# TensorE waits for its own last chunk, and makes a few narrow products, in every second up-projection chunk

## The reference

```python
for l in range(DEPTH):
    x = _layer_norm(DN_ALPHA * x + 0.5 * _swiglu(x, ffn1_w1[l], ffn1_w2[l]), ln1_g[l], ln1_b[l])
    mix = _token_mix(x, ...)
    x = _layer_norm(DN_ALPHA * x + mix, ln2_g[l], ln2_b[l])
    x = _layer_norm(DN_ALPHA * x + 0.5 * _swiglu(x, ffn2_w1[l], ffn2_w2[l]), ln3_g[l], ln3_b[l])
```

## Time and profile before

| | us |
|---|---|
| median of three runs | 2385.51 |
| lowest and highest | 2382.72, 2387.91 |
| profiled execution | 2399.49 |
| its span, first to last instruction | 2397.7 |
| TensorE busy | 2310.4 |
| VectorE busy | 1498.1 |
| ScalarE busy | 1190.8 |
| GpSimd busy | 244.1 |

### The profile page before, as it was taken

One profiled execution on the slowest core, in us unless ns is written; L12 is line 12 of the kernel. 1 busy time (PEld: TensorE's weight loads), 2 busy tenths in 40 slices (PEclk: granted clock), 3 DMA queues, 4 the chain that ended last, 5 costly groups with the idle time before them and its releaser, 6 DMA issues. The chain is left out here.

```text
span 2397.7 us, 45036 instructions
## 1 busy us (share of the span) xinstructions
PE 2310.4 (96%) x17296; PEld 2080.9 (87%) x17296; DVE 1498.1 (62%) x2663; ACT 1190.8 (50%) x1934; POOL 244.1 (10%) x272
## 2 busy tenths in 40 slices
PE   6999999999989999999999899999999998999998
PEld 4777677778878689999988899999999988999998
DVE  5487874453568875655476766655655578567654
ACT  6244743543345556434366555533534466555443
POOL 0012000000012000023010100121122001000320
PEclk9999999999999999999999999999999999999999
DMA  7321023444233035455554335455455454344552
GB/s 288 120 75 58 2 106 141 160 156 158 88 121 115 19 137 180 176 197 189 192 168 156 134 133 193 153 182 193 151 182 193 149 199 136 135 165 147 205 193 88
DMA packets 61844, 355.61 MB, mean 148 GB/s; under 512 B 6208, under 2 KB 19712, under 8 KB 20352
## 3 DMA queue, kind: packets, MB, share of 16 engines
q1 hardware_dynamic: 61552, 353.55, 41.0%
q10 hardware_dynamic: 144, 0.01, 0.0%
HBM read 349.29 MB, written 1.10 MB: 146 GB/s over the span
## 5 line engine op out<-in xcount | busy, mean ns | idle before, releaser
L240 DVE TENSOR_TENSOR w_lo<-ring,w_hi 128x1024 fp32r<-128x1024 f32 x638 | 811.9, 1305 | 454.7 <-ACT w_hi L226 454.3
L282 PE MATMUL psum<-x_hi,w_hi 128*128 128x256 f32 (+1 forms) x3376 | 1028.3, 305 | 13.2 <-DVE x_lo L579 3.6
L283 PE MATMUL psum<-x_lo,w_hi 128*128 128x256 f32 (+1 forms) x3376 | 1009.0, 299 | 0.0
L284 PE MATMUL psum<-x_hi,w_lo 128*128 128x256 f32 (+1 forms) x3376 | 1008.7, 299 | 0.0
L226 ACT ACTIVATE w_hi<-ring 128x1024 fp32r<-128x1024 f32 (+1 forms) x638 | 643.9, 1049 | 312.0 <-PE psum L284 145.5
L282 PEld LDWEIGHTS psum<-x_hi,w_hi 128*128 128x128 f32 x3376 | 638.1, 189 | 51.9 <-issue 12.0
L283 PEld LDWEIGHTS psum<-x_lo,w_hi 128*128 128x128 f32 x3376 | 636.7, 189 | 27.2 <-issue 1.7
L284 PEld LDWEIGHTS psum<-x_hi,w_lo 128*128 128x128 f32 x3376 | 635.3, 188 | 26.3
L1871 PE MATMUL psum<-h_hi,w_hi 128*128 (+1 forms) x640 | 179.0, 280 | 0.0
L1873 PE MATMUL psum<-h_lo,w_hi 128*128 (+1 forms) x640 | 179.0, 280 | 0.0
L1874 PE MATMUL psum<-h_hi,w_lo 128*128 (+1 forms) x640 | 179.0, 280 | 0.0
(11 more groups left out here) (332 smaller groups left out, 2859.1 us busy)
## 6 DMA issues: line engine op xcount, KB each, us to landing
ring<-wstream SPq DMA_DIRECT2D x320, 1024.0 KB, 4.8
x<-xT SPq DMA_DIRECT2D x2, 1024.0 KB, 7.7
x<-ctxT SPq DMA_DIRECT2D x2, 1024.0 KB, 10.2
rel_bias<-bias_by_distance SPq DMA_DIRECT2D x2, 1024.0 KB, 7.6
fox_bias<-forgetting_sums SPq DMA_DIRECT2D x2, 1024.0 KB, 7.5
cst<-consts SPq DMA_DIRECT2D x1, 1534.0 KB, 11.7
wk<-wk_once SPq DMA_DIRECT2D x8, 128.0 KB, 4.3
kk_sw<-kk_sw SPq DMA_DIRECT2D x8, 128.0 KB, 5.8
```

The lines of the kernel that those rows point to most:

```text
L240: dve.tensor_tensor(w_lo[:, c % 2, h], ring[:, (c + 2 * i) % RING, h], w_hi[:, c % 2, h].bitcast(F32), ALU.subtract).then_inc(split_done.s ...
L282: pe.matmul(o, w_hi[:, c, w_cols], hi, start=first, stop=False)
L283: pe.matmul(o, w_hi[:, c, w_cols], lo, start=False, stop=False)
L284: return pe.matmul(o, w_lo[:, c, w_cols], hi, start=False, stop=last)
```

## The change

In each up-chunk with s = 1 that `pe_columns` makes, TensorE waits, behind its two usual waits, until `chunk_done` counts its own chunk before. Then it makes `narrow` products of 32 columns with the first weight tile of the chunk and the first 32 tokens, into the accumulator's first 32 columns, which the first real product overwrites. `narrow` is 0 and 1 for the two feed-forward stages of the first layer and 2 and 3 for those of the second. Chunks with s = 0 and all other users of `pe_columns` get `None`, and for them nothing changes.

```diff
+NARROW = 32
...
-        def pe_columns(pe, i, s, hi, lo, tok, kt=KT, before=None, out=None, half_read=None):
+        def pe_columns(pe, i, s, hi, lo, tok, kt=KT, before=None, out=None, half_read=None, narrow=None):
...
                     if before and m == 0:
                         before(k)
+                    if narrow is not None and n == 0:
+                        pe.wait_ge(chunk_done.sem, g0[0] + s + 2 * i)
+                        for _ in range(narrow):
+                            pe.matmul(out[:, 0:NARROW], w_hi[:, c, 0:P], hi(0)[:, 0:NARROW], start=True, stop=True)
                     mm = three(pe, out[:, m * tok:m * tok + tok], slice(n * P, n * P + P), c, hi(k), lo(k), k == 0,
                                k == kt - 1)
...
-        def ffn_stage(layer, norm, more=True, bias=None):
+        def ffn_stage(layer, norm, more=True, bias=None, narrow=0):
...
-                                pe_columns(pe, i, s, hi, lo, S)
+                                pe_columns(pe, i, s, hi, lo, S, narrow=narrow if s else None)
...
-            ffn_stage(layer, layer_norm(layer - 1, 3) if layer else None, bias=None if layer else RelBias())
+            ffn_stage(layer, layer_norm(layer - 1, 3) if layer else None, bias=None if layer else RelBias(),
+                      narrow=2 * layer)
             mix_stage(layer)
-            ffn_stage(layer, layer_norm(layer, 2), layer < DEPTH - 1)
+            ffn_stage(layer, layer_norm(layer, 2), layer < DEPTH - 1, narrow=2 * layer + 1)
```

## The result

| | before | after |
|---|---|---|
| median of three runs, us | 2385.51 | 2410.89 |
| lowest and highest | 2382.72, 2387.91 | 2410.23, 2410.97 |
| profiled execution | 2399.49 | 2410.23 |
| its span | 2397.7 | 2408.5 |
| TensorE busy, products | 2310.4, 17296 | 2315.8, 17362 |

The change costs 25.4 us: ratio 1.0102, 95% interval 1.0067 to 1.0137. Forecast were 2407 (2389 to 2418), slower at 0.82.

What follows compares the result with a forecast made beforehand. TensorE, without a gap in the feed-forward stages, was taken to bound the kernel. To the median 2385.5 us were added 14.5 for waits and 7.3 for narrow products, with three long stages before and after: 2407.3, range 2389 to 2418.

Steps and rivals of the forecast that it cites:

- TensorE alone sets the end, and what is put into its queue is paid in full: Feed-forward stages: TensorE has no gap over 1584 products, about 180 to 187 us, so added work lengthens the stage.
- A wait costs 0.33 us: Up-chunks with s = 1: 44 waits at 0.33 us, 14.5 us together, ends 13.6 and 16.7.
- A narrow product costs 0.11 us: Behind the waits: 66 products paced by their loads at 0.11 us, 7.3 us together, ends 7.1 and 7.8.
- the 11 waits of one stage mostly come out alike: Feed-forward stages: supposed because each wait repeats the same sequence; a change of pace is worth 6.9 us a stage.
- a pace that varies from chunk to chunk within a stage: Feed-forward stages in the profile after: one of the signs named as showing the prediction wrong.
- Six in ten for long: Each feed-forward stage after the change: chance of the long pace, 0.1178 us a product against 0.1133.
- Three stages at the long pace before and three after: Four feed-forward stages: number of long ones unchanged, which one being indifferent, giving 2407.3 us; three long has chance 0.31.
- The first, waits that shake stages into the short pace: Feed-forward stages: two long 2400.4 us (chance 0.26), one 2393.5 (0.10), none 2386.6 (0.05).
- the fourth's two halves: Wait dearer, from 0.38 us, or timed runs before shorter-paced, from the 14 us: 2418 and more; "dearer" has chance 0.07.
- The second, all long: All four feed-forward stages become long, the fourth too: 2414.2 us, chance 0.11.
- The third, a pace below 0.1133: Feed-forward streams lock to 0.112 us a product, giving back 28.7 us: 2378.6, faster; chance 0.10.
- The fifth: The waits do nothing, the semaphore being always there before TensorE asks: 2385.5 + 7.3 us; given no chance.

Runs made afterwards that it cites:

- the four narrow products once: Kernel before plus four products of 32 columns, without a wait, ahead of one early chunk of each feed-forward stage; 2393.87 us, ratio 1.0028.

## Why the prediction was right, and where it wasn't

**TensorE alone sets the end, and what is put into its queue is paid in full: right.** All thirteen sums above charge every wait and every product at its full price. VectorE's and ScalarE's busy times differ from before by 0.3 and 1.1 us.

**A wait costs 0.33 us: right.** The hole is 0.33 in the earlier trace rows's counterpart after, and the third product behind it is late by 0.32 to 0.33, from a range of 0.31 to 0.38. That the new wait is met by the last product alone, and so stands nearer to ScalarE's release in the earlier trace rows than to the load in the earlier trace rows, held in the loop. In pairs that are written out the load came 0.39 to 0.40 after the last product, at the slow bound that the prediction took from the earlier trace rows, and the wait cost 0.40; those are five of 44.

**A narrow product costs 0.11 us: right.** The loads of the 66 are 0.108 to 0.112 apart, as those in the earlier trace rows. The Trainium skill's 25 ns for a product of 1 to 64 columns (TensorE: Matmul & The Clock Gate, Back-to-back issue gap) stands there for a product alone; the section says that in a stream of loads and products both set the distance. The trace agrees with that: where each product loads 128 columns of weights of its own, four to five times the 25 ns were measured.

**The stream keeps its pace, and "the 11 waits of one stage mostly come out alike": wrong.** This is the step that failed. A wait does not throw the dice for a stage; what comes out depends on what came in. In the loops a wait with none or two narrow products turned the pace every time, and one with three in 17 of 20 times, so the first, third and fourth stage of after alternate, with nearly half of their products long. A wait with one passed a short pace on, so the second stage was short. The prediction named a pace that varies from chunk to chunk within a stage as a sign that it is wrong, and that sign is there. "Six in ten for long" had counted seven restarts as if each were a draw; the rows said what paces exist, and not what an interruption does with them.

**"Three stages at the long pace before and three after": wrong on both sides, and the errors nearly met.** After, the long products of the profile are worth 8.9 us, 1.3 stages, not three. And the timed runs of before held fewer than its profile did. By the sum, the median of before is 2385.5 - 2377.8 = 7.7 us of long pace, 1.1 stages, and the median of after is 2410.9 - 2377.8 - 21.8 = 11.3, 1.6 stages. So the change took 21.8 for its own work and 3.6 through the pace, 25.4 together. The timed runs have no trace, so their stages are worked out and not seen; the traced ones say that the pace of before varies that way. The prediction had seen the 14.0 us between profile and median and named the right reason for it (two stages' worth), but held it no likelier than a cost of profiling. There is no such cost to be seen here: profiled executions fit the same sum, and several lie below their kernel's median (the four narrow products once: 2387.50 against 2393.87).

**The rivals.** The first, waits that shake stages into the short pace, is what the profile shows for one stage and half of three others; set against the profile before it is a gain of 11.4 us, as that rival has it, though the median was already short-paced. Of the fourth's two halves the dearer wait did not come, and the timed runs of before had fewer long stages, as it says; since after has few of them too, that was worth 3.6 us and not 14. The second, all long, did not come. The third, a pace below 0.1133, was seen in no stretch of such products (128 rows, 128 columns of weights, 256 columns) in any trace. The estimate of 109 ns from the Trainium skill's formula for a product alone (the same page and section) was not reached either. The fifth is out by the hole.

**What stays open.** Why a shift of the stream changes its pace. The runs show that the pace coming in and the size of the shift decide in nearly all cases (in the loops, none or two narrow products behind a wait turn it, three do in 17 of 20; without a wait, three or four narrow products or eight of constants turn it, and two brought it to the short pace within three trials in the five long streams of the traces and kept it there, but for the one trial behind the biases), that the wait isn't needed, and that a chunk's place in the ring isn't the cause. Two streams at the same pace need not answer alike to the same shift: three of 20 waits with three narrow products let a long pace pass, and one narrow product without a wait turned the pace five times of eleven. So the pace alone isn't the whole state of the stream. It was not seen what a wait with one narrow product does in the loop when the stream comes in long, why the kernel with one such wait in a stage came out short so often, nor what makes a stage of before start at one pace or the other.

## What to carry to other kernels

Where one engine is busy without a gap, added instructions can be priced from the nearest rows and summed, and here every sum held within 1.8 us; but first measure the distance of starts stage by stage, because a stream of equal products may have more than one pace and the difference (7 us a stage) can be as large as the change. A single profile is one draw of such a state: if it stands far from the median of the timed runs, count the state in both before taking a difference. When a stream has a good and a bad pace, a few cheap products early in the stream may settle it, as 24 narrow products in all, two at a time, did here in most runs.

## What the hardware showed that was not expected

- Products of 256 columns with a load of 128 columns each run at 0.1133 or 0.1178 us, with a clock of 1.00 at both; which of the two a stage starts with changes from execution to execution of the same program.
- A wait of TensorE on its own last product costs 0.32 to 0.33 us in a loop and 0.40 in pairs that are written out, where its load starts 0.39 to 0.40 after that product.
- Two narrow products ahead of every second chunk, 88 in all and worth 9.7 us, cost nothing against before (ratio 1.0002), because they hold all four stages at the short pace; three times a stage they gain 0.3%.
- A burst of four narrow products, or of eight products of constants, in an unbroken stream turned its pace six times of six, from short to long and from long to short.
